# Attention tile by tile, with half of the output projection and layer 0's conditioning products between its steps

## The reference

```python
def attend(q, k, v, mask=None, sink=None):
    s = jnp.einsum('bqhgd,bkhd->bhgqk', q, k).astype(jnp.float32) * (HEAD_DIM ** -0.5)
    if mask is not None:
        s = jnp.where(mask, s, NEG)
    m = jnp.max(s, axis=-1, keepdims=True)
    if sink is not None:
        sk = sink.astype(jnp.float32)[None, :, :, None, None]
        m = jnp.maximum(m, sk)
    e = jnp.exp(s - m)
    den = jnp.sum(e, axis=-1, keepdims=True)
    if sink is not None:
        den = den + jnp.exp(sk - m)
    p = (e / den).astype(v.dtype)
    return jnp.einsum('bhgqk,bkhd->bqhgd', p, v)
...
def reference(...):
    ...
    for l in range(DEPTH):
        need_ctx = l < DEPTH - 1
        sh1, sc1, g1, sh2, sc2, g2 = [m[:, None, :] for m in ada_params(c, ada_w[l], ada_b[l])]
        csh1, csc1, cg1, csh2, csc2, cg2 = ada_params(c_ctx, ada_w[l], ada_b[l])
        h = pre_mod(x, mix_pre_g[l], sh1, sc1)
        hc = pre_mod(xc, mix_pre_g[l], csh1, csc1)
        # l = 0: pooling mixer and windowed attention; l = 1: global attention; both end with "@ w_out"
        ...
        x = post_add(x, y, mix_post_g[l], g1)
        f = conv_ffn(pre_mod(x, ffn_pre_g[l], sh2, sc2), ffn_w_up[l], ffn_conv_w[l], ffn_conv_b[l], ffn_w_down[l])
        x = post_add(x, f, ffn_post_g[l], g2)
        ...                                   # layer 0 does the same for the context tokens
    return x
```

## Time and profile before

| | us |
|---|---|
| median of 3 runs | 1745.05 |
| lowest, highest | 1742.83, 1745.16 |
| profiled execution: time and span | 1741.7 |
| PE busy | 1544.9 (89%) |
| DVE, ACT, POOL busy | 1071.2, 726.3, 601.4 |

### The profile page before, as it was taken

How to read it: one execution, slowest core, us unless ns; L and a number is a source line. 1 busy time by engine, 2 the same in 40 slices (tenths; PEclk the granted TensorE clock), 3 DMA queues, 4 the chain that set the end, 5 groups by cost and what they waited for, 6 DMA issues and landing times.

```text
span 1741.7 us, 22126 instructions
## 1 busy us (share of the span) xinstructions
PE 1544.9 (89%) x7492; PEld 1233.1 (71%) x7492; DVE 1071.2 (62%) x1518; ACT 726.3 (42%) x1233; POOL 601.4 (35%) x507
## 2 busy tenths in 40 slices
PE   7759877778999999998999868779988799999998
PEld 1637666546888888887888657657766588888786
DVE  2776788766866777653335465668984544444455
ACT  3312367323433233322343443258774444443453
POOL 1324134134222222221333434434440444443344
PEclk9979889899999999999999989889999899999999
DMA  8341000441434554420112211100002133332222
GB/s 326 117 150 49 1 1 1 161 130 57 131 98 126 169 169 132 118 63 30 61 63 66 62 49 49 49 0 1 1 1 97 37 97 96 96 96 79 76 94 103
DMA packets 129132, 143.85 MB, mean 83 GB/s; under 512 B 7158, under 2 KB 95482, under 8 KB 129060
## 3 DMA queue, kind: packets, MB, share of 16 engines
q1 hardware_dynamic: 129060, 142.90, 26.0%
HBM read 140.79 MB, written 2.10 MB: 82 GB/s over the span
## 4 chain that ended last, share of the span: by engine, by line
PE 71%; DVE 13%; ACT 5%; issue 4%; POOL 3%; DMA 2%; SPq 0%; POOLq 0%; ACTq 0%; DVEq 0%
PE ps L358 20%; PE ps L359 20%; PE ps L360 19%; PE ps L1188 3%; PE ps L1174 2%; DVE hT_lo L696 1%; ACT prob L1215 1%; DVE ada_acc_proj L498 1%; DVE pT_lo L1274 1%; DVE o_tmp L1283 1%; PE ps L515 1%; DVE hT_hi L694 1%; POOL prob L1312 1%; DMA start_w<-in_ada_w_dram 1%; ACT o_tmp L1236 1%
## 5 line engine op out<-in xcount | busy, mean ns | idle before, releaser
L350 POOL TENSOR_TENSOR w_lo<-raw,w_hi 128x1024 fp32r<-128x1024 f32 (+1 forms) x196 | 386.3, 1974 | 724.9 <-ACT w_hi L343 724.9
L358 PE MATMUL ps<-hT_hi,w_hi 128*128 128x512 f32 (+1 forms) x1072 | 383.8, 358 | 16.4 <-DVE hT_lo L696 16.2
L359 PE MATMUL ps<-hT_lo,w_hi 128*128 128x512 f32 (+1 forms) x1072 | 381.5, 356 | 0.0
L360 PE MATMUL ps<-hT_hi,w_lo 128*128 128x512 f32 (+1 forms) x1072 | 378.9, 353 | 0.0
L343 ACT ACTIVATE w_hi<-raw 128x1024 fp32r<-128x1024 f32 (+1 forms) x208 | 181.3, 873 | 209.6 <-PE ps L360 175.7
L358 PEld LDWEIGHTS ps<-hT_hi,w_hi 128*128 128x128 f32 x1072 | 202.9, 189 | 56.6 <-DVE hT_lo L696 20.3
L360 PEld LDWEIGHTS ps<-hT_hi,w_lo 128*128 128x128 f32 x1072 | 202.2, 189 | 30.0
L359 PEld LDWEIGHTS ps<-hT_lo,w_hi 128*128 128x128 f32 x1072 | 202.8, 189 | 27.8
L1798 DVE TENSOR_TENSOR g_lo<-act_g,g_hi 128x768 fp32r<-128x768 f32 (+1 forms) x84 | 106.6, 1277 | 165.8 <-ACT g_hi L1748 164.6
L358 PE MATMUL ps<-w_hi,hT_hi 128*128 128x512 f32 (+1 forms) x368 | 147.7, 401 | 34.7 <-POOL w_lo L350 16.2
L358 PE MATMUL ps<-w_hi,g_hi 128*128 128x512 f32 x420 | 166.8, 397 | 3.5 <-DVE g_lo L1798 3.0
(11 more groups left out here) (178 smaller groups left out, 2452.2 us busy)
## 6 DMA issues: line engine op xcount, KB each, us to landing
raw<-in_ffn_w_up_dram SPq DMA_DIRECT2D x84, 512.0 KB, 3.8
ada_w_up<-in_ada_w_dram SPq DMA_DIRECT2D x48, 512.0 KB, 4.1
raw<-in_ffn_w_down_dram SPq DMA_DIRECT2D x84, 256.0 KB, 2.6
start_w<-in_ada_w_dram SPq DMA_DIRECT2D x8, 1024.0 KB, 9.8
ada_w_proj<-in_ada_w_dram SPq DMA_DIRECT2D x16, 512.0 KB, 4.1
ada_w_out<-in_ada_w_dram SPq DMA_DIRECT2D x16, 512.0 KB, 4.6
raw<-in_c_w_qkv_dram SPq DMA_DIRECT2D x12, 512.0 KB, 3.6
raw<-in_ab_w_in_dram SPq DMA_DIRECT2D x8, 512.0 KB, 5.3
```

What stands on the lines that cost most here:

```text
L350: by.tensor_tensor(w_lo[:, slot, 0:width], raw[:, n % RAW, 0:width], w_hi[:, slot, 0:width].bitcast(F32), ALU.subtract).then_inc(lo_split, 1)
L358: nc.tensor.matmul(outp, s_hi, m_hi, start=first, stop=False, skip_group_check=True)
L359: nc.tensor.matmul(outp, s_hi, m_lo, start=False, stop=False, skip_group_check=True)
L360: return nc.tensor.matmul(outp, s_lo, m_hi, start=False, stop=last, skip_group_check=True)
```

## The change

Groups now go tile by tile: all key heads of a query tile one after the other. The step list gets filler places F. In layer 0's attention these hold, in this order, 16 pairs A of conditioning products for blocks 2 to 5 (now matmuls with a 32-column stationary operand, straight from the loaded fp32 piece: four, one in each 32-row strip of a PSUM bank, by piece and column half), their folding Z, bias z, turning U and columns u, and the half-0 products W of the output projection for the 4 latent tiles, in portions of 6 matmuls. In layer 1's attention they hold 3 tiles in portions of 3 matmuls. H splits a half-0 weight unit (ACT, POOL), Y takes the product out of its bank (ACT). The filler has one PSUM bank, so that the output of attention has one bank instead of two. Conditioning on DVE in layer 0 is gone from both projections; its loads move to the start of attention. The output projection's half-0 weights are split in attention, and its remaining products rotate over 6 banks. The norm's semaphores are shared by all norms.

```diff
-        return [(j, n, list(range(ALL_T)), {}) for j in range(C_KV) for n in range(LAT_T)]
+        return [(j, n, list(range(ALL_T)), {}) for n in range(LAT_T) for j in range(C_KV)]
     out = []
-    for j in range(B_KV):
-        for n in range(LAT_T):
-            near = [m for m in (n - 1, n, n + 1) if 0 <= m < LAT_T]
-            out.append((j, n, ctx + near, {m: int(m > n) for m in near if m != n}))
-        out += [(j, n, ctx, {}) for n in ctx]
-    return out
-INTERLEAVE = ("S0 S1 E0 D0 C S2 E1 C D1 C C E2 S3 D2 C E3 D3 C".split(),
-              "S0 S1 E0 D0 C C S2 E1 D1 C C E2 S3 D2 C C E3 D3".split())
+    for n in range(LAT_T):
+        near = [m for m in (n - 1, n, n + 1) if 0 <= m < LAT_T]
+        out += [(j, n, ctx + near, {m: int(m > n) for m in near if m != n}) for j in range(B_KV)]
+    return out + [(j, n, ctx, {}) for n in ctx for j in range(B_KV)]
...
+INTERLEAVE = ("S0 S1 F E0 D0 C S2 E1 C F D1 C C E2 S3 F D2 C E3 D3 F C".split(),
+              "S0 S1 F E0 D0 C C S2 F E1 D1 C C E2 S3 F D2 C C E3 D3".split())
...
+OUT_DONE = (4, 3)
+def fill_ada():
+    at = {}
+    for p in range(ADA0_PAIRS):
+        at.setdefault(4 * (p // 3) + p % 3, []).append(("A", p, 0))
+    slot = max(at) + 1
+    at[slot] = [("P", 0, 0)]
+    for n, (half, what) in enumerate((h, w) for w in "ZU" for h in range(2)):
+        at[slot + 1 + 2 * n] = [(what, half, 0)]
+        at[slot + 2 + 2 * n] = [(what.lower(), half, 0)]
+    return at, slot + 9
...
+def fill_steps(l):
+    if l == 0:
+        at, slot = fill_ada()
+        at.setdefault(3, []).append(("H", 0, 0))
+        at.setdefault(7, []).append(("H", 1, 0))
+        at[slot - 8].append(("H", 2, 0))
+        at[slot - 6].append(("H", 3, 0))
+        for n in range(OUT_DONE[0]):
+            for u in range(4):
+                at.setdefault(slot + 5 * n + u, []).append(("W", n, (2 * u, 2 * u + 1)))
+            at.setdefault(slot + 5 * n + 4, []).append(("Y", n, 0))
+        return at
+    at = {3 * u + 1: [("H", u, 0)] for u in range(4)}
+    for n in range(OUT_DONE[1]):
+        first = 3 * (C_KV * n + 5) + 2
+        for k in range(KC):
+            at.setdefault(first + k, []).append(("W", n, (k,)))
+        at.setdefault(first + KC + 1, []).append(("Y", n, 0))
+    return at
...
+        def ada0_products(pe, p):
+            for n in (2 * p, 2 * p + 1):
+                pe.wait_ge(s(f"ada0_landed{n % ADA0_SLOTS}"), 16 * (n // ADA0_SLOTS + 1))
+            for n in (2 * p, 2 * p + 1):
+                m, k = 2 * (n // KC), n % KC
+                for half in range(2):
+                    r = 64 * (n % 2) + 32 * half
+                    mm = nc.tensor.matmul(ps[r:r + 32, FILL_BANK, :], cstat[:, k, C_AT - m:C_AT + 32 - m],
+                                          ada0_w[n % ADA0_SLOTS][:, half * BANK:(half + 1) * BANK],
+                                          start=p == 0, stop=p == ADA0_PAIRS - 1, skip_group_check=True)
+            mm.then_inc(s("ada0_mm"), 1)
...
+                    elif kind == "W":
+                        for k in i:
+                            if g == 0 and k % 2 == 0:
+                                wait_split(pe, f"out{l}", k // 2)
+                            if k == 0 and g:
+                                pe.wait_ge(s(f"mixpost{l}_ysq"), g)
+                            if k == 0 and g == 0 and l == 0:
+                                pe.wait_ge(s("ada0_columns"), 2)
+                            if k == (4 if l == 0 else 0):
+                                pe.wait_ge(s(f"o_split{l}"), 2 * per_tile * (g + 1))
+                            mm = out_half0(pe, l, g, k, bank(FILL_BANK))
+                        if i[-1] == KC - 1:
+                            mm.then_inc(s(f"mixpost{l}_acc"), 1)
...
-                    if i == 0 and g >= 2:
-                        pe.wait_ge(s(f"o_sum{l}"), 2 * (g - 1))
+                    if i == 0 and g:
+                        pe.wait_ge(s(f"o_read{l}"), 2 * g)
+                        pe.wait_ge(s(f"o_sum{l}"), 2 * g)
...
+                    elif kind == "Y":
+                        act.wait_ge(s(f"mixpost{l}_acc"), g + 1)
+                        first_half_scalar(act, f"mixpost{l}", four(bank(FILL_BANK)), y0_tile(l, g))
+                        act.wait_ge(s(f"mixpost{l}_y0"), g + 1)
+                        nc.scalar.activation(bank(FILL_BANK), bank(FILL_BANK), ACT.Square,
+                                             accum_out=ssum[:, 0, g:g + 1]).then_inc(s(f"mixpost{l}_ysq"), 1)
...
-                    dve.wait_ge(s(f"o_read{l}"), 2 * g + 2)
+                    dve.wait_ge(s(f"pv{l}"), first[g + 1])
+                    if g >= 2:
+                        dve.wait_ge(s(f"o_split{l}"), 2 * (g - 1))
+                    src = ps[0:HD, O_BANK, :].rearrange("p (a b n) -> p a b n", a=2, b=2)
                     for odd in range(2):
-                        rows = slice(64 * odd, 64 * odd + 64)
-                        src = ps[rows, 6 + g % 2, :].rearrange("p (a b n) -> p a b n", a=2, b=2)
-                        nc.vector.tensor_tensor(o_tmp[rows, g % 2, :, :], o_tmp[rows, g % 2, :, :], src[:, :, odd, :],
-                                                ALU.add).then_inc(s(f"o_sum{l}"), 1)
+                        nc.vector.tensor_copy(o_tmp[64 * odd:64 * odd + 64, g % 2, :, :],
+                                              src[:, :, odd, :]).then_inc(s(f"o_sum{l}"), 1)
...
-                    if l == 0 and m == 6:
-                        after_phase(sp, 3)
-                        ada_small_loads(sp, beside_proj, 0, (2, 3))
-                        ada_loads(sp, beside_proj, 0, 2 * KC)
...
+                if l == 0 and m == 3:
+                    after_phase(sp, 4)
+                    ada0_sync(sp)
                 load_unit(sp, f"out{l}", m, w[2 * u * P:(2 * u + 2) * P, half * BANK:(half + 1) * BANK]
                           .rearrange("(k p) n -> p k n", p=P), 1024)
-                if l == 0 and 2 <= m < 7:
-                    if m == 2:
-                        after_phase(sp, 5)
-                    more = 2 if m < 6 else 8
-                    ada_loads(sp, beside_out, n, n + more)
-                    n += more
-                    if m == 2:
-                        ada_small_loads(sp, beside_out, 0, (4, 5))
...
+            order = out_order(l, nt)
+            for i, (half, t) in enumerate(order):
+                if i >= len(OUT_BANKS):
+                    before_half, before_t = order[i - len(OUT_BANKS)]
+                    assert before_half == 0
+                    pe.wait_ge(s(f"{tag}_y0"), before_t + 1)
+                acc = bank(OUT_BANKS[i % len(OUT_BANKS)])
+                for k in range(KC):
+                    if half == 0:
+                        mm = out_half0(pe, l, t, k, acc)
+                        continue
```

421 lines of the change are left out of this document (245 added, 176 removed).

## The result

The changed kernel takes 1696.2 us (median of 4 runs, 1694.98 to 1697.08) against 1744.3 us for the kernel before in the same job: a ratio of 0.9731, 95% interval 0.9718 to 0.9744. That is 48 us faster where 61 were forecast; the time lies in the range of 1658 to 1712. The profiled execution's span is 1695.2 us, before 1741.7.

What follows compares the result with a forecast made beforehand. TensorE was taken as busy for most of each stage, with attention's waits around a ring with no engine full. Terms -28, -48.6, -16.4, +19 and +13 sum to -61: 1684 us, with an 8-in-10 range of 1658 to 1712.

Steps and rivals of the forecast that it cites:

- Term 1: Layer 0's input projection: conditioning sums and most of the wait for late w_lo weights go, -28 us.
- R5: Rival: the projection's waits stay because POOL's w_lo is the true bound; 1691 us, chance counted within the forecast's 0.50.
- Terms 2 and 3: Output projections: layer 0 does four products fewer, -48.6 us; layer 1 three fewer, -16.4 us.
- Term 5: Layer 1's attention: product portions +12, weight halves and copy-and-square pairs +2, single output bank 0; taken as +13 us.
- R4: Rival: slower than before, through waits for the single output bank at 26 boundaries; 1762 us at 3 us each, chance 0.05.
- Term 4: Layer 0's attention: takes in conditioning pairs, folds, turns and four output products, +19 us.
- Start and pairs: Layer 0's attention: first pieces arrive late, +7 us; 16 conditioning pairs at 0.77 us each, +2 us.
- R1: Rival: column strips run one after the other, so pairs cost more in layer 0's attention; 1697 us, chance 0.18.
- Folds and columns: Layer 0's attention: folds, bias and column work on DVE, itself full in a latent group, +4 us.
- Products: Layer 0's attention: four output products in 16 portions of 1.36 us, +9 us; +22 if all on the path.
- R2: Rival: filler nearly free since ring waits, not PE, set the period; 1665 us, chance 0.18.
- R3: Rival: filler fully on the path, +65 us instead of +32; 1717 us, chance 0.09.

Runs made afterwards that it cites:

- the bare kernel: Changed kernel with only the first of layer 0's 16 conditioning pairs and no output projection products in layer 0's attention: 1703.0 us, ratio 0.9772.

## Why the prediction was right, and where it was off

**Term 1 (-28, measured -29.4)** held as worked out. Nothing is left of PE's waits for conditioning sums, and the waits for POOL's w_lo fell from 11.0 us to 3.2. In the projection's waits after the change:

```profile
PE ps L462 <- POOL w_lo L454: 3.2, 6, 0.8
```

and before it:

```profile
PE ps L358 <- POOL w_lo L350: 11.0, 5, 8.2
```

R5 is refuted: POOL was late because the weights were issued late, not because it was full. That the number lies so close has some luck in it: by the starts of the next stage in all thirteen executions (173.5 to 177.5 us) it is -28 to -32.

**Terms 2 and 3 (-48.6 and -16.4, measured -48.3 and -16.1)** held. Counting a product at 24 matmuls of 0.2267 us was confirmed by an edit as well: four products moved back added 21.8 us to the output stage.

**Term 5 (+13, measured +18)** failed in one step: "I give it -1 to +1 a group and take 0", the single output bank. It costs 0.47 us a group, 7.7 us in all. A group with filler took 11.18 us, as forecast (11.2); but a group without took 10.31 and not 9.8, so the products themselves were dearer in the forecast (12) than on the chip (8.5). The mis-sized bank was partly covered by a price on the other side. The splits with the copies and squares were put at 2; the splits, with the order, took 1.8. (The parts of this term add up to 14 in the prediction, which then takes 13.) The reasoning set a wait of 0.7 us against PE's slack of 0.9 in a group. But that slack was no free time at the place of the wait: it consists of PE's waits at other steps of the ring. With one bank and with two, both without filler, over layer 1's stage:

```profile
PE ps L1360 <- DVE o_tmp L1459: 10.5, 15, 1.0
```
```profile
PE ps L1349 <- DVE pT_lo L1451: 4.6, 17, 0.4
```

The single bank brings 10.5 us of waits. Those for DVE's copy shrink from 4.6 to 1.0, those for ACT (9.8 to 9.2) and POOL (5.7 to 6.0) stay, so about 7 us come on top. R4 named the mechanism and asked 3 us a group for its verdict; the place was right, the size a sixth.

**Term 4 (+19, measured +31.6)** failed in the same step and in smaller ones:
- Start and pairs, forecast 7 + 2. Taking 15 pairs away gave 7.0, and a wait of 4.6 us for the first piece stayed: 11.6 in all. The wait of all pieces was 7.3 us, as forecast; the pairs were dearer, 1.07 us instead of 0.77. A five-key group's PE work rose by 3.2 us to 11.55, over the 10.6 that the forecast gave, and became the bound.
- The 0.444 us by which a pair was priced is the time of one record. The order of PE's instructions has four to a pair, as the old sum has in the kernel, and the trace eight records: each of these fp32 matmuls leaves two. A 32-column matmul takes 0.89 us, a pair in series 3.55, side by side 0.89 at the least. With this the forecast for R1, pairs one after the other, would have been far higher, and the measured 1.07 is close to the lower end and not to the middle.
- Folds and columns, forecast 4. The group that holds them takes 13.6 us in the bare kernel too, the next four-key group there 9.1: 4.5. These are not the folds' alone: the same group holds two weight splits and a held DVE operation, and cutting the splits took 1.24 us off it.
- Products, forecast 9, measured 5.7.
- The output bank, forecast 0. In the bare kernel PE waits for it 10.7 us in 8 places. The prediction did not price it in this stage at all. With 4.6 for the first piece and 4.5 for the fold group this makes 19.8 for the 19.1 us that remain over the stage before. The sum fits, but only part of it was tested: moving DVE's read ahead gave 3.1 us in layer 0, and no run has two output banks there. So the bank as the cause is shown in layer 1 and argued in layer 0. The key order, the clock (forecast -3; granted 0.85 before, 0.94 after, 0.84 in the bare kernel) and the held DVE operations lie in the same 19 us, and were not separated from the bank there.

R2 (filler nearly free) is refuted by the stages, +50 against its +13, although in layer 0 the products came cheaper than forecast; R3 (fully on the path) by layer 0's products, 5.7 us on the path of 21.8. The likeliest case, with its own range of 1670 to 1698, was the right one, if only just: 1696.2 stands 2 us inside it, and stands near R1's 1697, whose mechanism did not happen. The number alone could not have told the two apart.

The Trainium skill's rule in "TensorEngine Tiling (Array Packing)", key properties, that a change of tiling mode drains TensorE, was weighed in the prediction at +13 by the rule and +1 by the row. The changed kernel's timeline around a pair bears out the row:

```profile
224.56 0.28 PE L1340 MATMUL ps<-mask_b,ident_b 128*128 128x128 bf16 x2
224.77 1.06 PE L1252 MATMUL ps<-ada_w,cstat 128*32 128x512 f32 x8
225.77 0.66 PE L1349 MATMUL ps<-ident,prob 128*128 128x128 f32 x4
```

The next instruction starts 1.00 us after the pair does, and no idle time stands on either side. What a record's columns take is read from the old sum, whose weight loads follow one another at 0.43 us (the prediction's 0.437 stands in no row):

```profile
355.27 0.11 PEld L515 LDWEIGHTS ps<-ada_acc_out,select 128*32 128x32 f32 x1 [0.32 <-issue]
355.70 0.11 PEld L515 LDWEIGHTS ps<-ada_acc_out,select 128*32 128x32 f32 x1 [0.32 <-issue]
```

Two records in each strip are 0.86 us, so that at most 0.14 us a pair can be a drain, about 2 us for all 16.
